# Left-over rows of a mixture-of-experts block: down projection in four 32-column strips, and routed sums kept in two tensors

## The reference, cut to what matters

```
    idx, w = _route(xt, router_w, router_bias)
...
        gu = x_pad[rows] @ w_gu[e]
        y = ((jax.nn.silu(gu[:, :f]) * gu[:, f:]) @ w_down[e]) * rw[:, None]
        return acc.at[rows].add(y)
...
    return (routed + shared).reshape(B, L, D)
...
        h = _layer_norm(ALPHA * h + ffn, ln_gain[i, 1], ln_bias[i, 1])
```

## Time and profile before

| | us |
|---|---|
| median of three runs | 1253.17 |
| lowest, highest | 1250.25, 1254.72 |
| the profiled execution | 1256.82 |
| its span, first to last instruction | 1255.0 |
| PE busy / DVE / POOL / ACT | 1189.5 / 787.9 / 606.0 / 420.8 |
| mean granted TensorE clock | 0.985 of full |
| DMA | 317.50 MB |

### The profile page before, as it was taken

How to read it: one execution, slowest core, us unless ns; L and a number is a source line. 1 busy time by engine, 2 the same in 40 slices (tenths; PEclk the granted TensorE clock), 3 DMA queues, 4 the chain that set the end, 5 groups by cost and what they waited for, 6 DMA issues and landing times.

```text
span 1255.0 us, 22626 instructions
## 1 busy us (share of the span) xinstructions
PE 1189.5 (95%) x7122; PEld 1040.6 (83%) x7122; DVE 787.9 (63%) x1625; ACT 420.8 (34%) x582; POOL 606.0 (48%) x509
## 2 busy tenths in 40 slices
PE   6999999999999799999999999999999999999973
PEld 6897989747874399999999999999999998998931
DVE  7565657388988256666665566566566655647528
ACT  5253435353441023233333233233232232323323
POOL 5222222001657455666555666666666665756310
PEclk9999999999999999999999999999999999999997
DMA  6111111403352979999999999999999999999864
GB/s 240 51 35 51 44 41 34 184 27 135 102 169 71 278 230 352 375 364 359 370 355 366 357 351 362 358 349 367 344 352 355 343 352 338 346 350 341 282 165 175
DMA packets 83587, 317.50 MB, mean 253 GB/s; under 512 B 15989, under 2 KB 32450, under 8 KB 58594
## 3 DMA queue, kind: packets, MB, share of 16 engines
q1 hardware_dynamic: 56592, 249.50, 51.4%
q0 software_dynamic: 26656, 67.23, 21.9%
q10 hardware_dynamic: 306, 0.34, 0.1%
HBM read 274.38 MB, written 51.00 MB: 259 GB/s over the span
## 4 chain that ended last, share of the span: by engine, by line
DMA 50%; PE 24%; issue 11%; DVE 9%; ACT 3%; POOL 3%; POOLq 1%; DVEq 0%; ACTq 0%; SPq 0%
DMA routed_rows<-ysb,to_row 47%; PE bank L116 6%; PE bank L117 6%; PE bank L118 6%; PE bank L957 3%; PE bank L440 2%; POOL expert_list L787 1%; DMA win_raw<-in_w_in 1%; POOL routed_rows L840 1%; DVE routed L1440 1%; DVE h L1136 1%; DVE routed L1429 1%; DMA lists<-expert_list 1%; DVE h L1134 1%; DVE h L1120 1%
## 5 line engine op out<-in xcount | busy, mean ns | idle before, releaser
L957 PEld LDWEIGHTS bank<-xT,wgu 128*128 128x128 f32 x4096 | 516.3, 192 | 21.2 <-issue 10.4
L957 PE MATMUL bank<-xT,wgu 128*128 128x160 f32 (+1 forms) x4096 | 521.0, 288 | 10.5 <-DVE xT L1317 9.6
L810 POOL DMA_INDIRECT xg<-h_rows,from_row x288 | 324.2, 1126 | 110.6 <-issue 86.7
L840 POOL DMA_INDIRECT routed_rows<-ysb,to_row x96 | 147.8, 1540 | 215.8 <-issue 210.3
L1098 ACT ACTIVATE ysb<-bank,of_row 128x512 f32<-128x512 f32 x64 | 44.0, 687 | 439.3 <-DVE to_row L1312 381.1
L1359 DVE TENSOR_TENSOR wd_lo<-wd_raw,wd_hi 128x1024 fp32r<-128x1024 f32 x128 | 151.1, 1222 | 39.9 <-ACT wd_hi L1089 39.4
L1089 ACT ACTIVATE wd_hi<-wd_raw 128x1024 fp32r<-128x1024 f32 x128 | 127.9, 1048 | 1.4 <-issue 0.6
L787 POOL DMA_INDIRECT expert_list<-entry,place x64 | 64.7, 1010 | 129.9 <-DVE place L1197 112.2
L116 PE MATMUL bank<-hT_hi,win_hi 128*128 128x348 f32 (+1 forms) x320 | 113.4, 355 | 9.7 <-DVE hT_lo L538 9.7
L352 POOL TENSOR_TENSOR win_lo<-win_raw,win_hi 128x1024 fp32r<-128x1024 f32 x16 | 43.6, 2725 | 145.6 <-ACT win_hi L463 145.5
L1302 DVE TENSOR_TENSOR picks<-lists,pick 128x20 f32<-128x20 f32 x64 | 11.9, 185 | 161.5 <-POOLq L834 111.0
(11 more groups left out here) (216 smaller groups left out, 1629.5 us busy)
## 6 DMA issues: line engine op xcount, KB each, us to landing
wgu<-in_w_gu SPq DMA_DIRECT2D x128, 1024.0 KB
wd_raw<-in_w_down SPq DMA_DIRECT2D x64, 1024.0 KB, 8.4
win_raw<-in_w_in SPq DMA_DIRECT2D x16, 512.0 KB, 3.9
xg<-h_rows,from_row POOLq DMA_INDIRECT x288
hT_raw<-in_hT SPq DMA_DIRECT2D x8, 520.0 KB, 7.4
wout_raw<-in_w_out SPq DMA_DIRECT2D x1, 4096.0 KB, 14.4
h_in<-in_h_rows SPq DMA_DIRECT2D x8, 512.0 KB, 4.0
h_rows<-h SPq DMA_DIRECT2D x8, 512.0 KB, 2.7
```

Source lines behind the costliest of these rows:

```text
L810: pool.indirect_dma_start(out=xg[b][:, g, :], out_offset=None, in_=h1_quarters, in_offset=bass.IndirectOffsetOnAxis(ap=from_row[b][:, g:g ...
L840: pool.indirect_dma_start(out=routed_rows, out_offset=bass.IndirectOffsetOnAxis(ap=to_row[b][0:r, half:half + 1], axis=0), in_=ysb[b][0:r, ...
L957: mm = pe.matmul(bank[:, 2 * f + half, 0:BLOCK[b]], wgu[b][:, f, k, c:c + P], xT[b][:, k, 0:BLOCK[b]], start=(k == 0), stop=(k == KT - 1))
```

## The change

- **Strips.** The left-over rows get a tensor of their own, `hid_rest` (plain float32, 128 x 2 x 32), written by one DVE multiply for each f; the extra columns of `hid_hi` and L1335 go. PE takes them after the 12 matmuls of the block: for each c and k one plain float32 matmul, 32 stationary and 512 moving columns, straight from `wd_raw`, each into its own 32 partitions of PSUM (`rest_at`: (c, k) at 32 * (2c + k)). There are four instead of eight, and they don't accumulate: ACT copies the k = 1 strip to `y_rest`, DVE adds the k = 0 strip. `wd_lo` of even blocks moves to another address, since `wd_raw` must live on.
- **Two tensors.** Even blocks add into `routed_rows[0]`, which starts as `h1` as before, odd ones into `routed_rows[1]`, which starts as zeros: POOL fills `zeros` (128 x 512) early in the mixer and issues one DMA that writes all 4 MB from it, in 2,048 pieces of 2 KB. The store of block t, and the evacuation into `ysb[b]`, now wait for the store of block t-2. `ysb_free` is gone; ACT and DVE wait for `y_stored[b]` themselves.
- **End.** SP loads both tensors, sixteen tiles: the eight of tensor 0 when its last store has landed, the eight of tensor 1 after that. DVE adds the shared sums into tensor 0 (`add_shared`, six tiles ahead), then tensor 1 with the sum for the mean (`add_small`, eight more passes over 128 x 1024).
- The four memsets of `hid_hi` and `hid_lo` on POOL go.

```
-                for c in range(2 if REST[b] else 0):
-                    if first:
-                        pe.wait_ge(y_dve, YS[1] + before(YS, i, j))
-                    pe.matmul(bank[:, 6 + c, :], hid_hi[b][:, k, P:2 * P], w[c][0],
-                              start=first, stop=False)
-                    mm = pe.matmul(bank[:, 6 + c, :], hid_hi[b][:, k, P:2 * P], w[c][1],
-                                   start=False, stop=last)
...
+            if REST[b]:
+                pe.wait_ge(y_dve, YS[1] + before(YS, i, j))
+            for c in range(2 if REST[b] else 0):
+                for k in range(FT):
+                    at = rest_at(c, k)
+                    mm = pe.matmul(bank[at:at + REST[b], 6 + c, :], hid_rest[:, k, :],
+                                   wd_raw[b][:, k, c * 512:(c + 1) * 512],
+                                   start=True, stop=True)
+                mm.then_inc(down_done, 1)
...
-            pool.wait_ge(y_stored[1 - b], stores_to(i, j - 1))
-            pool.sem_inc(ysb_free, 1)
+            pool.wait_ge(y_stored[b], stores_to(i, j - 2))
...
-            act.wait_ge(ysb_free, t + 1)
+            act.wait_ge(y_stored[b], stores_to(i, j - 2))
...
+        s.step(pool.memset(zeros[:, :], 0.0))
+        pool.dma_start(routed_rows[1].rearrange("(p i) (c d) -> p (i c) d", p=P, c=2),
+                       zeros[:, :].unsqueeze(1).to_broadcast([P, 2 * TILES, D // 2])
+                       ).then_inc(y_stored[1], 16)
...
+        for b in range(2):
+            sp.wait_ge(stores_done, b + 1)
+            for j in range(TILES):
+                sp.dma_start(routed[b][:, j, :], routed_rows[b][cols(j), :]
+                             ).then_inc(routed_ready[b][j], 16)
...
+        def add_small(n):
+            b, x = n % 2, routed[0][:, n, :]
             dve.wait_ge(sh_read, n + 1)
+            dve.wait_ge(routed_ready[1][n], 16)
+            dve.scalar_tensor_tensor(x, x, 1.0, routed[1][:, n, :], ALU.mult, ALU.add,
+                                     accum_out=mean2[b][:, 0:1]).then_inc(tail_add, 1)
```

More of the change, by code:

```diff
@@ L130, in build @@
     expert_list = nc.dram_tensor("expert_list", (LIST, 2), F32).ap()
-    routed_rows = nc.dram_tensor("routed_rows", (SEQ, D), F32).ap()
+    routed_rows = [nc.dram_tensor(f"routed_rows{b}", (SEQ, D), F32).ap() for b in range(2)]
     sched_dram = nc.dram_tensor("sched_dram", (P, 4), I32).ap()
@@ L194, in build @@
     th = m.at("th", 191488, [P, LT, LP], F32)
+    zeros = m.at("zeros", 200000, [P, D // 2], F32)
     pads = m.at("pads", 191488, [P, LIST_COLS, 2], F32)
@@ L220, in build @@
     wd_raw = [m.at(f"wd_raw{j}", wd_at[j], [P, FT, D], F32) for j in range(2)]
-    wd_lo = [m.at(f"wd_lo{j}", wd_at[j], [P, FT, D], F32R) for j in range(2)]
+    wd_lo = [m.at(f"wd_lo{j}", (166432, wd_at[1])[j], [P, FT, D], F32R) for j in range(2)]
     wd_hi = [m.at(f"wd_hi{j}", wd_hi_at[j], [P, FT, D], F32R) for j in range(2)]
     sg = m.at("sg", 49152, [P, FT, SEQ], F32)
-    y_rest = m.at("y_rest", 49152, [P, 2, 512], F32)
+    y_rest = m.at("y_rest", 49152, [P, 512], F32)
     sh = m.at("sh", 57504, [P, FT, SEQ], F32)
@@ L227, in build @@
     xT = [m.at(f"xT{j}", 85536 + 6144 * j, [P, KT, SQ * GB[j]], F32) for j in range(2)]
-    hid_hi = [m.at(f"hid_hi{j}", (129152, 96416)[j], [P, FT, 2 * P], F32R) for j in range(2)]
+    hid_hi = [m.at(f"hid_hi{j}", (129152, 96416)[j], [P, FT, P], F32R) for j in range(2)]
+    hid_rest = m.at("hid_rest", 130176, [P, FT, REST[0]], F32)
     hid_lo = [m.at(f"hid_lo{j}", (131200, 98464)[j], [P, FT, P], F32R) for j in range(2)]
@@ L239, in build @@
     ranked_i = m.at("ranked_i", 127808, [P, 5, E], I32)
-    hid = m.at("hid", 127808, [P, FT, BLOCK[0]], F32)
+    hid = m.at("hid", 127808, [P, FT, P], F32)
     ysb = [m.at(f"ysb{j}", 149376 + 8192 * j, [P, 2, D], F32) for j in range(2)]
-    routed = m.at("routed", 0, [P, TILES, D], F32)
+    routed = [m.at(f"routed{b}", (0, 132992)[b], [P, TILES, D], F32) for b in range(2)]
     consts_ready = sem("consts_ready")
@@ L634, in build, with rest_at @@
     silu_ready, hid_ready, hid_step = sem("silu_ready"), sem("hid_ready"), sem("hid_step")
-    y_act, y_dve, ysb_free = sem("y_act"), sem("y_dve"), sem("ysb_free")
+    y_act, y_dve = sem("y_act"), sem("y_dve")
     halves = lambda a: a.rearrange("p (c t) -> p c t", c=2)
+    def rest_at(c, k):
+        return (2 * c + k) * SQ
     def before(counts, i, j):
@@ L643, in stores_to @@
     def stores_to(i, j):
-        return loads(i, j) * STORES[j % 2] + 16 * (j % 2)
+        return loads(i, j) * STORES[j % 2] + 16
     def loads(i, j):
@@ L657, in build @@
     y_rest_ready = sem("y_rest_ready")
-    routed_ready = [sem(f"routed_ready{i}") for i in range(TILES)]
+    routed_ready = [[sem(f"routed_ready{b}_{i}") for i in range(TILES)] for b in range(2)]
     sh_down_done, sh_read = sem("sh_down_done"), sem("sh_read")
@@ L840, in experts_pool @@
                 pool.indirect_dma_start(
-                    out=routed_rows,
+                    out=routed_rows[b],
                     out_offset=bass.IndirectOffsetOnAxis(ap=to_row[b][0:r, half:half + 1],
@@ L1370, in experts_dve @@
                 hidden(i, j + 1, 1)
-            dve.wait_ge(ysb_free, t + 1)
+            dve.wait_ge(y_stored[b], stores_to(i, j - 2))
             dve.sem_inc(dve_pass, 1)
@@ L1378, in experts_dve @@
                 dve.wait_ge(y_rest_ready, before([2 * (r > 0) for r in REST], i, j) + c + 1)
+                at = rest_at(c, 0)
                 dve.scalar_tensor_tensor(
-                    ysb[b][0:REST[b], 1, c * 512:(c + 1) * 512], bank[0:REST[b], 6 + c, :],
-                    of_row[b][0:REST[b], 1, 1:2], y_rest[0:REST[b], c, :], ALU.mult, ALU.add
-                    ).then_inc(y_dve, 1)
+                    ysb[b][0:REST[b], 1, c * 512:(c + 1) * 512],
+                    bank[at:at + REST[b], 6 + c, :],
+                    of_row[b][at:at + REST[b], 1, 1:2], y_rest[at:at + REST[b], :],
+                    ALU.mult, ALU.add).then_inc(y_dve, 1)
         dve_steps.append(s.n)
     def last_sp(sp):
-        sp.wait_ge(stores_done, 1)
-        for j in range(TILES):
-            sp.dma_start(routed[:, j, :], routed_rows[cols(j), :]).then_inc(routed_ready[j], 16)
+        for b in range(2):
[3 more added lines that the diff above has]
+                             ).then_inc(routed_ready[b][j], 16)
         for i in range(TILES):
             sp.wait_ge(out_ready, i + 1)
-            sp.dma_start(out[cols(i), :], routed[:, i, :]).then_inc(out_stored, 16)
+            sp.dma_start(out[cols(i), :], routed[0][:, i, :]).then_inc(out_stored, 16)
         sp.wait_ge(out_stored, 16 * TILES)
@@ L1410, in last_act @@
             act.wait_ge(mean2_ready, n + 1)
-            act.activation(h1[:, n, :], routed[:, n, :], ACT.Square,
+            act.activation(h1[:, n, :], routed[0][:, n, :], ACT.Square,
                            bias=mean2[b][:, 1:2], accum_out=var2[b][:, 0:1]
@@ L1443, in finish @@
                                      ALU.mult, ALU.add).then_inc(out_ready, 1)
-        add_shared(0)
+        for n in range(TILES - 2):
+            add_shared(n)
+        add_small(0)
         dve.wait_ge(lnf_loaded, 16)
@@ L1448, in last_dve @@
             if n + 1 < TILES:
-                add_shared(n + 1)
+                add_small(n + 1)
+            if n < 2:
+                add_shared(TILES - 2 + n)
             finish(n)
```

61 lines of the change are left out of this document (28 added, 33 removed).

## The result

| | before | after |
|---|---|---|
| median of 20 runs each, us | 1252.23 | 1257.93 |
| lowest to highest, us | 1248.56 to 1257.87 | 1254.21 to 1262.75 |
| profiled span, us | 1255.0 | 1258.8 |
| first up product starts at | 439.87 | 439.21 |
| loop: from there to the start of the last 160-column up product | 731.0 | 728.7 |

The changed kernel is slower by 0.42%: ratio 1.0042, 95% interval 1.0028 to 1.0056, or +5.7 us. The forecast said +14. Its sign was right and its reason was not: in the two profiled executions the loop even gained 2.3 us, and the loss, 6.8 us, lies in the end. Each profile is one execution.

A forecast was written before the change was run, and what follows sets the result against it. Matmuls were taken to bound the loop until some 700 us, then the store chain. Loop +11, start +3 and end 0 gave +14 on 1253.17, so 1267 us; range 1230 to 1282, the forecast's own 1253 to 1276.

The forecast's parts named there:

- What bounds the kernel now: Opening step on the loop: matmuls bound it until some 700 us at 23.28 us a pair, then the chain of stores.
- After that the store chain does: Loop after some 700 us: adding stores, one after the other, bound it by 0.44 us a pair.
- Part 1: Stores in the loop: two tensors take their chain off the path, from 23.58 to PE's 23.28, 0.30 us a pair.
- Part 2: Strips in the loop: they cost 2.5 us against 1.88 removed, so PE's pace becomes 23.9 us a pair.
- five slots: Strips' eight records, starting in program order, overlap only partly: 5 x 0.436 = 2.18 us; the slower forecast, chance 0.44.
- the change of shape: PE's switch into the strips and out of them: between nothing and 0.7 us, taken as 0.35 us.
- all four side by side: Strips on PE all overlap, each with two records in sequence: 0.87 us, or 1.2 us with the switch of tiling.
- Rival 3: Loop: strips overlap but the DMA engines bound it, 23.3 to 23.5 us a pair; most likely 1250 us, chance 0.12.
- rival 2: Loop: all strips overlap and it gets faster, between 22.6 and some 23.1 us a pair; 1233 us, chance 0.30.
- Part 3: Start: POOL's issue of 2,048 pieces of zeros makes PE idle, 3 us taken, with 0 to 4.3 allowed.
- Part 4: End: store wait saved, 4 MB more loaded, first pass over tensor 1 at 1217.5; together 0 us, between -3 and +4.
- The sum: Whole kernel: +11 us for the loop, +3 for the start, 0 for the end; +14 on the median of 1253.17.

The follow-up runs named there:

- after_less_load: Changed kernel with six of eight parts of every up weight loaded in the loop, 1 MB a pair left out; 1229.59 us, ratio to before 0.9806.
- after_one_strip: Changed kernel with all four left-over products of an even block on the same 32 array columns and 32 partitions; 1309.00 us, ratio to before 1.0449.
- tensors_alone: Changed kernel with its two tensors and end, but the earlier kernel's eight left-over products in place of the strips; 1261.25 us, ratio to before 1.0068.
- after_strips_twice: Changed kernel with the four strips' products issued twice into the same places; 1261.52 us, ratio to before 1.0068.
- strips_alone: Kernel before with the four strips added, keeping its one tensor of routed sums and chain of stores; 1257.10 us, ratio to before 1.0033.

## Why the prediction was wrong, step by step

- **What bounds the kernel now.** "A pace so even ... is PE's own": right, for the first part of the loop. "After that the store chain does": wrong. The DMA engines were the bound of the loop as a whole, behind the chain. I took the early weights as slack: loads land 9.7 us after issue. In the kernel before the weights stay early to the end (8.1 us between 720 and 1150 us); what comes late there is the stores, for which the rest waits. Without the chain the weights take the stores' place: in the changed kernel a load of `wd_raw` lands after 9.1 us (median, 450 to 520 us) and later after 16.5 (586 to 1110 us), and ACT waits for it. The slower PE, the longer its pace lasts: with two tensors 5 to 6 pairs at 22.57, 17 at 23.28 and 24 at 23.42; with the chain 7 at 22.57 and 9 to 11 at 23.28. The sum is 726 to 732 us in all ten kernels that have all bytes and adding stores and a PE pace below the DMA engines'. The share of 1.02 could not have told me: `after_less_load` and `after_one_strip` have 0.98 to 1.03 and run at PE's pace.
- **Part 1.** The chain went, but not to PE's pace: -0.30 us a pair was expected, `tensors_alone` shows 0.
- **Part 2, the term that made the forecast.** This is the step that failed: the strips were to cost five slots, 2.18 us, and 0.35 for the change of shape, 2.53 us a pair; measured 1.00 from the first strip record to the next up product, and 22.57 - 21.40 = 1.17 by PE's pace. That is the case "all four side by side", 0.87 us and 0.3 for the change of shape. The row on which I chose (all records start in program order) was about products on all columns and said nothing on strips. PE's pace at first is 22.57, where this case gave 22.6. But it was not only the size: even 1.2 us would not have given the time, since PE's pace was not what the loop as a whole follows. The Trainium skill, TensorE: Matmul & The Clock Gate, Part 3: Packing small matmuls, says that matmuls keep program order in start and end. For these records of one float32 product the trace differs: four of eight start together at 809.02, which program order with two records a strip would not allow. Its span model gave the right size. The change of shape: L118 and the first strip start 0.31 us apart, where two rounded products start 0.23 apart; behind the strips some 0.13 us remain beside the two records; and the up product that follows takes 8.69 us, not 8.59. Together 0.3 us, and `after_strips_twice`, which has one change of shape for two sets, agrees: its second set costs 0.85 where the first costs 1.17.
- **Rival 3** said what happened in the loop: strips side by side and the DMA engines as the bound, a pace of 23.3 to 23.5. It was 728.7 / 31 = 23.50. Its time, most likely 1250, was short by about the end's 7 us. I gave it 0.12, with "loads aren't waited for" against it. For rival 2 I took 375 GB/s, the fastest slice, as a rate that the loop could hold; in the changed kernel it is 365 between 600 and 700 us and 348 between 900 and 1000. Bytes a second were the wrong measure besides, since packets of adding stores took twice the time of plain ones (327 against 159 ns).
- **Part 3.** +3 us expected, about 0 measured: POOL's issue of 2,048 pieces took 1.21 us, near the lower bound. The second `win_lo` begins 2.3 us later than before (20.89 against 18.56), within the 2.5 us of room, and PE has no gap there; after its next wait it goes on at 64.95 against 64.84. The first up product starts 0.66 us earlier than before, which is within the spread of the start.

```profile
16.78 1.21 POOL L381 DMA_DIRECT2D routed_rows<-zeros  x1 [0.32 <-POOL zeros L380]
```

- **Part 4.** 0 us expected, between -3 and +4; measured +6.8. The store of block 63 did go 7.2 us sooner by the clock of the trace (1201.45 against 1208.62), but 3.1 of them are the earlier loop; counted from the last 160-column up product it is 4.1 us. What I had left out: DVE must work off six `add_shared` ahead of the first `add_small`, and the last three wait for PE, whose product for all tiles starts late, behind a gap that the chain had hidden, and behind 12 products at the lower clock. So the first pass came at 1221.60 where the working had 1217.5; its tile landed at 1219.09.
- **The sum.** -0.7 for the start, -2.3 for the loop, +6.8 for the end: +3.8 between the profiled spans, +5.7 between the medians. +14 was the wrong term for the loop (+11, measured -2.3) and for the start (+3, measured -0.7, no more than noise). These two errors pointed up, the third, in the end, pointed down and made good a part of them. The right sign was luck: it came from the end, which I had put at 0.

## What to carry to other kernels

A pace that is even and full on one engine can still be paid from a lead: before spending a gain on PE, find out what the DMA engines need over the whole loop. A DMA share near 1.0 doesn't tell (0.99 here in a loop that PE bounds as well). One cut of the bytes (an eighth of the traffic left out) does, in one run: if the loop gets shorter or its even pace lasts longer, the bytes were the bound. And when a chain of waits is removed, read again all gaps that it had covered, above all at the end, where nothing else covers them.

## What the hardware showed

- Four products on four strips of 32 columns, 512 columns streamed, plain float32: 8 records in 1.07 us, against 3.62 us for the same eight on one strip. With the way in and out the set costs PE 1.17 us, a second set behind it 0.85.
- An adding indirect store costs the DMA engines clearly more than a plain one of the same packets: 21.8% against 15.7% of the span for that queue, 2.55 us of 16 engines a pair of blocks, 3.5 by the row of `after_less_load`; 327 against 159 ns for the median 4 KB packet.
- TensorE's clock: a gap of 3.43 us kept the full level in the kernel before, gaps of 4.00 us (changed kernel, 0.77 and then 0.55) and of 2.85 us (`strips_alone`, 0.66) did not. So the length of the gap alone doesn't decide; what else does these runs don't show.
- DVE's SBUF-only pass takes 3.24 us instead of 1.28 beside POOL's add.
